# A two-layer hybrid block on one core: the first transfers held back, the columns moved into the memory's piece, and the split of the memory tiles given to VectorE alone

## The reference

```
def rms_norm(x, g):
    y = x * lax.rsqrt(jnp.mean(x * x, axis=-1, keepdims=True) + EPS)
    return y * g

def hybrid_layer(x, mem, ...):
    h = rms_norm(x, norm_pre)                    # x: 256 tokens x 1024
    proj = h @ w_in                              # sb_q, sb_k, ml_i/f, sb_v, sb_z, ...
    ...
    mkv = rms_norm(mem, mem_norm) @ w_mem_kv     # mem: 256 x 1024
    mem_k, mem_v = jnp.split(mkv, 2, axis=-1)
    ...
```

## Time and profile before

| | us |
|---|---|
| median of 3 runs | 1752.31 |
| the profiled execution | 1751.61 |
| its span (first to last instruction) | 1749.8 |
| PE busy | 1734.2 (99%) |
| DVE busy | 1307.9 (75%) |
| ACT busy | 1017.4 (58%) |

### The profile page before, as it was taken

One profiled execution on the slowest core, in us unless ns is written; L12 is line 12 of the kernel. 1 busy time (PEld: TensorE's weight loads), 2 busy tenths in 40 slices (PEclk: granted clock), 3 DMA queues, 4 the chain that ended last, 5 costly groups with the idle time before them and its releaser, 6 DMA issues.

```text
span 1749.8 us, 24255 instructions
## 1 busy us (share of the span) xinstructions
PE 1734.2 (99%) x9136; PEld 1495.1 (85%) x9136; DVE 1307.9 (75%) x1747; ACT 1017.4 (58%) x1406; POOL 99.6 (6%) x154
## 2 busy tenths in 40 slices
PE   8999999999999999999999999999999999999998
PEld 7888888888888888888889988888888988888887
DVE  6787767665877786756669787688778987678775
ACT  5676656454666755644555765755556656555544
POOL 1000000000000000000000000500003360000000
PEclk9999999999999999999999999999999999999999
DMA  9755655566765565565666554456555515356563
GB/s 303 205 156 175 181 159 166 165 187 190 248 183 161 172 181 170 156 181 169 192 194 198 182 192 157 144 182 192 191 186 188 170 37 181 121 168 189 188 189 108
DMA packets 211028, 308.70 MB, mean 176 GB/s; under 512 B 11808, under 2 KB 114848, under 8 KB 210656
## 3 DMA queue, kind: packets, MB, share of 16 engines
q1 hardware_dynamic: 208640, 299.44, 55.5%
q0 software_dynamic: 2128, 7.66, 1.3%
q10 hardware_dynamic: 144, 0.05, 0.0%
HBM read 306.06 MB, written 1.05 MB: 176 GB/s over the span
## 4 chain that ended last, share of the span: by engine, by line
PE 93%; DVE 3%; ACT 2%; issue 1%; DMA 0%; SPq 0%; DVEq 0%; ACTq 0%
PE bank L1701 51%; PE bank L1766 26%; PE bank L1733 3%; PE bank L2168 3%; PE bank L2217 2%; DVE weights_lo L1050 1%; PE bank L1816 1%; PE bank L1830 1%; PE bank L2089 1%; PE bank L2107 1%; PE bank L1799 1%; ACT weights_hi L570 1%; PE bank L1838 0%; DVE arena L1104 0%; DMA weights_raw<-in_w_mem_kv_dram 0%
## 5 line engine op out<-in xcount | busy, mean ns | idle before, releaser
L1050 DVE TENSOR_TENSOR weights_lo<-weights_raw,weights_hi 128x1024 fp32r<-128x1024 f32 x560 | 668.3, 1232 | 222.4 <-ACT weights_hi L570 216.7
L570 ACT ACTIVATE weights_hi<-weights_raw 128x1024 fp32r<-128x1024 f32 x559 | 574.4, 1056 | 395.6 <-DMA weights_raw<-in_w_in_dram 188.0
L1701 PE MATMUL bank<-weights_hi,h_parts 128*128 128x512 f32 x1856 | 567.5, 391 | 0.3 <-DVE h_parts L1482 0.2
L1701 PEld LDWEIGHTS bank<-weights_hi,h_parts 128*128 128x128 f32 x1856 | 348.0, 188 | 73.3 <-DVE h_parts L1482 0.6
L1701 PE MATMUL bank<-weights_lo,h_parts 128*128 128x512 f32 x928 | 347.5, 389 | 0.0
L1766 PE MATMUL bank<-h_parts,weights_hi 128*128 128x512 f32 (+1 forms) x1248 | 302.7, 384 | 0.9 <-DVE arena L1104 0.8
L1701 PE MATMUL bank<-weights_hi,arena_parts 128*128 128x512 f32 x928 | 269.9, 390 | 0.0
L1766 PEld LDWEIGHTS bank<-h_parts,weights_hi 128*128 128x128 f32 x1248 | 219.8, 189 | 40.5 <-DVE arena L1104 1.5
L1701 PEld LDWEIGHTS bank<-weights_lo,h_parts 128*128 128x128 f32 x928 | 174.3, 188 | 35.4
L1701 PEld LDWEIGHTS bank<-weights_hi,arena_parts 128*128 128x128 f32 x928 | 173.6, 188 | 35.4 <-ACT arena L590 0.2
L1766 PEld LDWEIGHTS bank<-h_parts,weights_lo 128*128 128x128 f32 x1248 | 169.4, 190 | 11.1
(11 more groups left out here) (306 smaller groups left out, 1629.4 us busy)
## 6 DMA issues: line engine op xcount, KB each, us to landing
weights_raw<-in_w_in_dram SPq DMA_DIRECT2D x224, 512.0 KB, 3.7
weights_raw<-in_f_w_up_dram SPq DMA_DIRECT2D x96, 512.0 KB, 3.5
weights_raw<-in_f_w_down_dram SPq DMA_DIRECT2D x48, 512.0 KB, 3.6
weights_raw<-in_w_up_dram SPq DMA_DIRECT2D x40, 512.0 KB, 3.6
weights_raw<-in_c_w_pw_dram SPq DMA_DIRECT2D x24, 512.0 KB, 3.6
weights_raw<-in_ab_w_in_dram SPq DMA_DIRECT2D x20, 512.0 KB, 3.7
weights_raw<-in_w_out_dram SPq DMA_DIRECT2D x16, 512.0 KB, 3.8
weights_raw<-in_xa_wk_dram SPq DMA_DIRECT2D x16, 512.0 KB, 3.4
```

Source lines behind the costliest of these rows:

```text
L570: nc.scalar.activation(w_hi[:, q % SPLIT, 0:w], raw[:, n % RAW, 0:w], ACT.Copy).then_inc(hi_done, 1)
L1050: tt(w_lo[:, n % RAW, 0:w], raw[:, n % RAW, 0:w], w_hi[:, q % SPLIT, 0:w].bitcast(F32), ALU.subtract)\
L1701: return mm(bs[t][:, :], sp_[:, 2 * u + kk, t * P:(t + 1) * P], wp[:, kk, :], start=first and u == us[0] and kk == 0 and n == 0, stop=last ...
```

## The change

1. The 104 columns become the first columns of the memory's first piece: `first_rows` is 128 x (104 + 2048), piece 0 is 128 x 616, and ScalarE's own transfer is gone.
2. SyncE holds its first transfers: piece 2 waits for piece 0, unit 1 for the first half of unit 0, unit 2 for the second half, unit 3 for piece 2, the token tiles and unit 4 for unit 1, unit 5 for unit 2.
3. VectorE makes both parts of all eight memory tiles; ScalarE makes weight parts only.
4. Ten matmuls on zeros, where there were six.
5. `mrs` stands behind `sbz` in both layers, on TensorE, on ScalarE and in the table that deals the banks.

```diff
-        memT = sb("mem_features", [P, KD, S])
+        first_rows = sb("mem_features", [P, C_MEM + KD * S])
+        cols, memT = first_rows[:, 0:C_MEM], first_rows[:, C_MEM:].rearrange("p (k s) -> p k s", k=KD)
...
             def mem_piece(i):
                 k0, k1 = MEM_PIECES[i]
-                sp.dma_start(memT[:, k0:k1, :], A["memT"][:, k0:k1, :]).then_inc(memT_in[i], 16)
+                a, b = (C_MEM + k0 * S if i else 0), C_MEM + k1 * S
+                sp.dma_start(first_rows[:, a:b], A["memT"][:, a:b]).then_inc(memT_in[i], 16)
...
                 if n == 1:
+                    sp.wait_ge(memT_in[0], 16)
                     mem_piece(2)
+                    sp.wait_ge(first_in, 16)
+                if n == 2:
+                    sp.wait_ge(raw_full[0], 16)
+                if n == 3:
+                    sp.wait_ge(memT_in[2], 16)
                 if n == 4:
+                    sp.wait_ge(raw_full[1], 16)
                     for t, s in enumerate((x0_in, x1_in)):
...
+                if n == 5:
+                    sp.wait_ge(raw_full[2], 16)
...
                 if l == 0:
-                    act.dma_start(cols[:, :], A["columns"]).then_inc(cols_in, 16)
                     log_exp_table()
-                    hi = M_HL["L0"][0]
-                    act.wait_ge(cols_in, 16)
-                    for i, (k0, k1) in enumerate(MEM_PIECES):
-                        up_to(i + 1)
-                        if i == 0:
-                            continue
-                        act.wait_ge(memT_in[i], 16)
-                        for k in range(k0, k1):
-                            link(nc.scalar.activation(hi[:, k, :], memT[:, k, :], ACT.Copy, scale=cols[:, 8 + k:9 + k]), f"m_hi{k}")
                     up_to(5)
...
-                    dve.wait_ge(cols_in, 16)
                     for i, (k0, k1) in enumerate(MEM_PIECES):
                         dve.wait_ge(memT_in[i], 16)
                         for k in range(k0, k1):
-                            if i:
-                                dve.wait_ge(act_done, SC.at(f"m_hi{k}"))
-                            else:
-                                link(ts(hi[:, k, :], memT[:, k, :], cols[:, 8 + k:9 + k], None, ALU.mult))
+                            link(ts(hi[:, k, :], memT[:, k, :], cols[:, 8 + k:9 + k], None, ALU.mult))
                             link(stt(lo[:, k, :], memT[:, k, :], cols[:, 8 + k:9 + k], hi[:, k, :].bitcast(F32),
                                      ALU.mult, ALU.subtract), f"m_lo{k}")
-                        up_to(i + 1)
+                        if i:
+                            up_to(i)
...
-                    idle(6)
+                    idle(10)
...
                 proj_T("sbv")
+                proj_T("sbz")
                 pe.wait_ge(act_done, SC.at("mem.rstd1"))
                 b = begin("mrs")
...
                 end(ins, "mrs")
-                proj_T("sbz")
```

More of the change, by code:

```diff
@@ L137, in build @@
         ident_r = sb("ident_parts", [P, P], F32R)
-        cols = sb("vector_columns", [P, 104])
         cols2 = sb("vector_columns_2", [P, 616])
@@ L158, in build @@
         ident_in, const_in, x0_in, x1_in, mem_in = (sem(n) for n in ("ident_in", "const_in", "x0_in", "x1_in", "mem_in"))
-        cols_in, pos_in, bif_in, cols2_in, mem2_in = (sem(n) for n in ("cols_in", "pos_in", "bif_in", "cols2_in", "mem2_in"))
+        pos_in, bif_in, cols2_in, mem2_in = (sem(n) for n in ("pos_in", "bif_in", "cols2_in", "mem2_in"))
         brow_in, win_in, ws_in, out_done = (sem(n) for n in ("brow_in", "win_in", "ws_in", "out_done"))
@@ L234, in build @@
             ORDER[f"L{l}"] = (four("mk") + (two("mv") if l == 0 else []) + four("hT") + four("sbq") + four("sbk") + pick("mlif", 0)
-                              + two("sbv") + pick("mrs", 0) + two("sbz") + (two("mv") if l else []) + four("sbs") + four("mlq") + four("mlk") + four("sbw") + two("mlv")
+                              + two("sbv") + two("sbz") + pick("mrs", 0) + (two("mv") if l else []) + four("sbs") + four("mlq") + four("mlk") + four("sbw") + two("mlv")
                               + pick("mle", 0) + four("mld") + two("sby", "mlo", "mlz") + four("mls") + two("rtq", "rtk") + four("mly")
@@ L500, in _ @@
                     pool.wait_ge(vec_done, VC.at("n_lo3", "L0"))
-                    pool.dma_start(memT[:, :, :], A["mem_2T"]).then_inc(mem2T_in, 16)
+                    pool.dma_start(first_rows[:, C_MEM:], A["mem_2T"]).then_inc(mem2T_in, 16)
                     pool.wait_ge(vec_done, VC.at("res", "L0"))
@@ L716, in layer @@
                                               ACT.Sin), "trig")
+                for t in range(NT):
+                    copy(tok(3)[:, t, :], "sbz", t, ACT.Silu, f"sbz{t}")
                 b = filled("mrs")
                 link(nc.scalar.activation(junk[:, 0:S], b[:, 0:S], ACT.Copy), ("free", "mrs", 0), "mrs")
-                for t in range(NT):
-                    copy(tok(3)[:, t, :], "sbz", t, ACT.Silu, f"sbz{t}")
                 if l:
@@ L2236, in build @@
     return [C.marks for C in (PC, SC, VC, GC)]
+C_MEM = 52 * DEPTH
 COL_AB, COL_C, COL_F = 0, 80, (376, 496)
@@ L2244 @@
         "c_w_pw2_2", "c_b_pw2_2", "xa_wq_2", "xa_wk_2", "xa_wv_2", "xa_wo_2", "f_w_up_2", "f_w_down_2", "final_norm_2"]
-_LAID = ["memT", "mem_2T", "columns", "columns_2", "gm_wsT", "constants", "windows"]
+_LAID = ["memT", "mem_2T", "columns_2", "gm_wsT", "constants", "windows"]
 def columns(np, rows):
@@ L2253, in feature_major @@
 def feature_major(np, m):
-    return np.reshape(m.T, (KD, P, S)).transpose(1, 0, 2)
+    return np.reshape(m.T, (KD, P, S)).transpose(1, 0, 2).reshape(P, KD * S)
 def laid_out(np, inputs):
@@ L2267, in laid_out @@
         second += [I["xa_norm_2"][l], I["xa_mem_norm_2"][l], I["f_norm_2"][l], I["f_dw_w_2"][l], I["f_dw_b_2"][l]]
-    got = {"memT": feature_major(np, I["mem"][0]), "mem_2T": feature_major(np, I["mem_2"][0]), "columns": columns(np, first),
+    got = {"memT": np.concatenate([columns(np, first), feature_major(np, I["mem"][0])], 1), "mem_2T": feature_major(np, I["mem_2"][0]),
            "columns_2": columns(np, second), "gm_wsT": np.transpose(I["gm_ws"], (0, 3, 1, 2)),
```

## The result

| | before | changed |
|---|---|---|
| median | 1752.37 us (1752.08 to 1752.50, 4 runs) | 1773.15 us (1772.79 to 1775.57, 4 runs) |
| the profiled execution's span | 1749.8 us | 1771.4 us |

The ratio is 1.0122, with the interval [1.0104, 1.0139]: the change made the kernel 20.8 us slower. The forecast was 1749.9, with 1751.8 as the upper end of the range, and no rival went beyond 1753.7.

What follows compares the result with a forecast made beforehand. TensorE, 93% of the chain, was taken as the bound, with its 5.7 us wait at the head to be gained from. -2.36 us at the token stage plus 0 for `mrs` took 1752.31 to 1749.9 us, range 1748.3 to 1751.8.

Steps and rivals of the forecast that it cites:

- step 4: At the token stage: unit 9's landing holds ScalarE's `h_parts` to 34.85, so 2.36 of 3.57 us get through.
- the slower one: Rival: the holds let the DMA stream run dry, `h_parts` starts 1.4 us later than before: 1753.7 us, chance 0.08.
- Step 1: At the head: VectorE makes tiles 0-7, so unit 1's low matmuls start at 14.85 instead of 18.42, 3.57 us earlier.
- The hole of 2 us: TensorE's wait for VectorE before unit 1's low matmuls, replacing a 5.7 us hole and 3 us at half clock.
- the rival of a fallen clock: The clock falls in the head's new hole, costing 1.7 us at half speed: 1750.4 us, chance 0.20.
- a late landing: Rival: piece 2 or unit 1 lands late at the head, VectorE's chain loses 1.9 us: 1750.6 us, chance 0.13.
- Step 2: At the head: ten matmuls on zeros end at 8.0 to 9.9 us and cost nothing.
- Step 3: At the head: SyncE's holds lose 0 to 0.5 us of the DMA stream, with 0.2 us taken.
- DMA share under 0.9 between 6 and 20 us: A sign, at the head, that the forecast is wrong: DMA engines not busy all the time.
- TensorE's wait of 1.2 us: A new wait ahead of TensorE's first token matmul, some 1.2 us, released by ScalarE's `h_parts`.
- no cap: Rival: the held stream brings unit 9 1.2 us earlier, all 3.57 us get through: 1748.3 to 1748.7 us, chance 0.17.
- Step 5: Moving `mrs` behind `sbz` removes a 0.42 us wait, but the chain behind keeps its time: 0, bounds -0.4 to +0.1 us.

Runs made afterwards that it cites:

- idle_6: The changed kernel with the old addresses (memory's tile and row vectors exchanged), with six matmuls on zeros instead of ten: 1748.93 us, ratio 0.9983 to before.
- after_old_addresses: The changed kernel with the allocations of the memory's tile and the row vectors exchanged, so the weights lie where they lay: 1748.88 us, ratio 0.9982 to before.
- no_holds: after_old_addresses with SyncE's six waits taken out, so the first transfers are issued at once: 1747.83 us, ratio 0.9975 to before.
- scalar_no_holds: after_old_addresses without SyncE's six waits and with ScalarE making the high parts of tiles 2 to 7 again: 1751.19 us, ratio 0.9994 to before.

## Why the prediction was wrong

**Part 1, the columns in the memory's piece: the step that failed.** It was priced as a transfer only: "308 KB instead of 256 KB is ... 0 to 0.8 us; I take 0.1 us". That the tile grows by 416 bytes, and that the buffers allocated behind it move, was not looked at. It costs 24.3 us (1773.15 - 1748.88). With it fell the sentence of step 4 that "with no wait over 0.8 us in the rest of the run the shift stays to the end": there was indeed no such wait, but a list of waits cannot show matmuls that all take 7 ns longer. A rival for this was not among the four; the slower one was about the transfers.

The Trainium skill's page "SBUF — State Buffer", section "SBUF: two separate sides", has it that PE never waits on anyone for SBUF. This case's trace agrees as far as other engines go: the 234 ns stand in quiet moments too. The Trainium skill's page "TensorE: Matmul & The Clock Gate", section "Step-by-step: what each phase is for", has it that the load of the next weights takes no read bandwidth from the running matmul, since TensorE has two independent read ports. By that the distance between the two operands would be free, and here it is not: 391 against 398 ns, and the measurement decides. That the two reads of TensorE hold each other up is a reading that fits and is not shown; what shows is only the distance.

**Step 1** was right in kind, and 1.1 us too late. The columns with piece 0 landed sooner, not later, than alone; VectorE's timeline:

```profile
3.84 0.35 DVE L1171 TENSOR_SCALAR arena_parts<-mem_features 128x256 fp32r<-128x256 f32 x1 [2.70 <-DMA mem_features<-in_memT_dram]
...
12.46 2.36 DVE L1050 TENSOR_TENSOR weights_lo<-weights_raw,weights_hi 128x1024 fp32r<-128x1024 f32 x2
```

The start was taken as 5.05 and was 3.84: the 308 KB landed 3.0 us after their issue, and no cost of the rows' odd starts shows. From there the sum holds: low part of unit 1 at 12.46 against 13.5 forecast, the low matmuls at 13.73 against 14.85. The hole of 2 us with VectorE as its releaser became two small ones, 0.98 us released by ScalarE, which had waited for unit 1 to land, and 0.30 by VectorE, which decides. The clock stayed at 1.00: the rival of a fallen clock, given 0.20, did not come, nor did that of a late landing: unit 1 was split at 10.21, well ahead of 13.5.

**Step 2** was right in its price: 0, by idle_6. Its times were not: the matmuls on zeros end at 7.55, where 8.0 to 9.9 was named. The slow spacing of the first ones is also no 0.50 in the granted clock, as the hole's was; both traces show 1.00 in every microsecond from 1 to 9, so what makes them slow stays open.

**Step 3** had the right sign and was too small. 0.2 us was taken and 0.5 was the upper end; the stream is 1.89 us later at unit 9 by the holds (after_old_addresses against no_holds), and 1.1 us are left of it in the span. "DMA share under 0.9 between 6 and 20 us" was named as the sign of an error, and in the changed kernel it is there:

```profile
10.00:11.00 1.00, 0.34 (x3) 0.14 (x2) 0.92 (x3) 0.79 (x1) 0.00 (x0) 1.00 0.73 226
...
12.00:13.00 1.00, 1.00 (x6) 0.82 (x5) 0.96 (x2) 0.73 (x1) 0.00 (x0) 1.00 0.81 285
```

**Step 4** had the right numbers, and that was luck. ScalarE's rows in the changed kernel:

```profile
32.27 1.06 ACT L580 ACTIVATE weights_hi<-weights_raw 128x1024 fp32r<-128x1024 f32 x1 [0.43 <-DMA weights_raw<-in_w_in_dram]
...
34.65 1.49 ACT L661 ACTIVATE h_parts<-bank,mem_features 128x256 fp32r<-128x256 f32 x3 [0.20 <-PE bank L1827]
```

Unit 9 is split at 32.27 (forecast near 32.5) and `h_parts` starts at 34.65 (34.65 to 34.85). That the landings do not depend on where TensorE stands is what scalar_no_holds shows. But "the same absolute time" was wrong: 32.37 is the latest of eleven traces with the old head, the others have 30.22 to 31.73. (The issues ahead of unit 9 add up to some 9 MB, too, not 8.) Unit 9 is at 31.95 to 32.60 in the six traces with the holds, and at 30.20 and 30.12 in the two without: two things cancel, a late execution that the forecast was read from, and the holds, priced at 0.2.

Nor is unit 9 what caps the head of the changed kernel. ScalarE's `h_parts` row waits 0.20 us for TensorE. TensorE's wait of 1.2 us is there, but it stands earlier than forecast: at the memory's values, on VectorE's low part behind the late unit 4 (1.17 us of the 1.4 at L1698). The rival "no cap", with 1748.3 to 1748.7, is close to what happens without part 2: ScalarE's `h_parts` starts at 32.98 in no_holds, where 33.6 was named, and the time is 1747.83 us. It was argued for from the holds; it is the case without them.

**Step 5** was right; after_old_addresses:

```profile
34.93 1.93 PE L1763 MATMUL bank<-h_parts,weights_hi 128*128 128x256 f32 x8
...
85.88 2.09 PE L1763 MATMUL bank<-h_parts,weights_hi 128*128 128x512 f32 x8 [0.66 <-ACT arena L600]
...
97.47 2.08 PE L1763 MATMUL bank<-h_parts,weights_hi 128*128 128x512 f32 x8 [0.17 <-DVE arena L1104]
```

From 34.93 to 97.47 are 62.54 us. Before, from 37.83 to the 100.37 of the earlier trace rows, it is 62.54 too: the exchange at `mrs` brought nothing.

**The sum** without part 1's addresses: -2.4 forecast; 2.6 in the spans (1749.8 to 1747.2), and 0.9982 [0.9973, 0.9991] of before, or 1.6 to 4.7 us, by the runs. So near a sum is in part luck: step 1 was 1.1 us too late, step 3 too small, and step 4 rested on a late execution. What was not in the sum at all is the 24 us.

## What to carry to other kernels

When a change alters the size of a buffer, compare the addresses of everything behind it in the two built programs, and price the pair that the hot matmuls read: here 7 ns on each of 2784 matmuls and a little on the others were 24 us, against a gain of some 3 us. When a kernel gets slower and no wait has grown, put the mean ns of each group, by shape, beside those of before; put beside them a control pair whose distance was kept. Before a forecast rests on the time of one landing, look at it in several executions: here it moved by 2 us. Transfers held back to put them in order pay only if the trace shows that the DMA engines stay busy meanwhile; here they brought nothing, and cost about 1 us between two kernels.

## What the runs showed of the hardware that was not expected

- A 128x512 matmul with the weights streaming takes 391 to 398 ns by the distance in SBUF between its two operands alone (567.4 and 580.2 us for 1856 of them); over this kernel 0 to 24 us of 1752. Equal distances modulo 256 bytes gave equal times. It needs no other engine and no transfer: from start to start 234 against 227 ns, in quiet moments as over all. Why some distances are slow stays open: the runs fix neither the bits of the address that count nor which of the two reads is held up.
- The sign of the effect depends on the shape: with `h_parts` streaming, the 128x256 matmul took 282 ns at distance 0 and 277 at 64, and the 128x512 one 393 and 396. With the weights streaming, the 128x512 one took 391 and 393. At 192 only the weights' streaming is slow (397 against 393).
- The landing of unit 9, which is split on arrival, moves from one execution to the next: eleven traces with the same head have the split at 30.22 to 32.37 us.
- A piece of 308 KB with rows of 8608 bytes was landed and in use at 3.84 us; the columns' own small transfer released VectorE only at 4.95.
